# Masked queries as weights for the decode states, and page queues written out with another order of requests

## The chip, the cores and the metric

One Trainium2 chip, one of its cores. TensorE does matmuls into PSUM, DVE (VectorE) and ACT (ScalarE) do elementwise work, POOL (GpSimd) and SP (SyncE) mostly issue DMAs here. The metric is the device time of one launch in microseconds.

## The reference

One step of a small decoder trunk with two layers, for a prompt of 512 tokens and, with the same weights, for 8 decode sequences of 4 new tokens each. Every layer is a half-weighted SwiGLU, a mixer and a second half-weighted SwiGLU, each behind an RMS norm. Two parts of the mixers matter here.

The even mixer holds an mLSTM with 4 heads of width 192. For a decode sequence it has a state matrix per head. With a the decay of a token, s the weights of the sequence's own new tokens, and den the normaliser:

```
num = einsum('bhts,bhse->bhte', s, vc) + a[..., None] * einsum('bhed,bhtd->bhte', c, qc)
h   = num / maximum(abs(den), exp(-mt))[..., None]
c_new = decay[..., None, None] * c + einsum('bhs,bhse,bhsd->bhed', wk, vc, kc)
```

The odd mixer is a sparse attention over 2048 past tokens, kept in pages of 128 rows that a page table points to; a row holds `[cmp_k, cmp_v, sel_k, sel_v]`. The compressed branch averages overlapping blocks of the cmp rows, scores them, and its probabilities choose the 16 blocks that the selected branch may see; a third branch sees a window of the last 512 rows.

## The kernel before, in words

All five engines run programs written out by hand, with semaphores between them; nothing plans the order but the order of the code.

**Decode states.** `pe_even_decode`, `act_even` and `dve_even` go over 32 states (n = 8 x head + sequence). A state is 192 x 192, held as 96 rows of 2 x 192. For each state TensorE transposes it with four 96 x 96 transposes into PSUM bank n % 2 (`flip_state`, L1155), two states ahead; ACT copies the result to `cT` (L1323, three buffers); TensorE then multiplies it with the four scaled queries of that sequence (L1200): the transposed state is the weights, the queries are four moving columns, and the product lands in PSUM bank 7, channels in partitions, beside the terms of the new tokens (L1171) that were put there first over zeros (L1164). L1173 and L1176 make the denominators in bank 2. Every four states, eight matmuls on four row tiles (L1193) form the update of four states, and DVE adds each to its decayed state (L1456), which GpSimd stores (L905). Behind the loop L1206 does the normaliser state n, DVE multiplies the numerators with `rdn` (L1459), and the output projection starts (L939).

The fp32 matmuls of this kernel appear as two instructions each in the profile, the transposes as one.

**Pairs of sequences.** `pe_odd` takes the 8 decode sequences in four pairs (`pe_pair`, i = 0 to 3). Of the pages of a pair, SP loads those of the first sequence and GpSimd those of the second, 16 pages each, and of each page three parts apart: cmp rows (128 KB), selected keys (64 KB) and selected values (64 KB); GpSimd also loads the windows. One buffer holds one pair, so a part is asked for again when it has been read: the cmp rows after `pe_compress_pair` (L1921, counted by `sums_done`), the keys after the flips of the selected keys (L1949, `tk_done`), windows and values after the last product (L2011, `pvs_done`). TensorE's order within pair i is: scores of compressed rows, five flips of keys with their scores (L1949, L1972; the fifth reads the windows), then the compression of pair i+1 (L1921) with its transposes (L1928), then the transposes of the probabilities (L1989) and the products with the values (L2006, L2011). DVE picks the blocks and masks (L2269 to L2286); ACT takes the exponential (L2117), and does the copies for the compression of pair i+1 (L2098, L2100) ahead of the exponential of the selected scores.

The two queues before run this loop (GpSimd's, in `pool_odd`; SP's in `load_keys` is the same without the windows):

```python
            with po.Fori(0, NB // 2 - 1) as i:
                page = page_numbers(po, i + 1, 1)
                po.wait_ge(sums_done, i + 1)
                # cmp rows of pair i + 1
                po.wait_ge(tk_done, i * 5 + 4)
                # selected keys of pair i + 1
                po.wait_ge(pvs_done, i + 1)
                # windows, then selected values, of pair i + 1
```

`page_numbers` reads 16 entries of the page table into registers (L1686); its address is computed from the loop register. The first pair's numbers are read by SP one at a time at fixed addresses (L1707). `load_page` is L1691, `load_windows` L1697.

Of the kernel before, what the change touches and what calls it, by code (L numbers as in the profile page):

```python
# [22 lines left out]
SEQ = 512  # L23
# [47 lines left out]
def make_consts():  # L71
# [21 lines left out]
    put("onehot4", np.eye(4))  # L93
    put("round_mask", ((p[:, None] % 32) // NT == 4 * np.arange(2)[None, :] + p[:, None] // 32))
# [82 lines left out]
def trunk(nc, x_prompt, x_sample, state_pool, state_mlstm_c, state_mlstm_n, state_mlstm_m,  # L177
# [6 lines left out]
    with ctx:  # L184
# [530 lines left out]
        cT = [hf[:, 384 * i:384 * i + 384].rearrange("p (d e) -> p d e", d=2) for i in range(3)]  # L715
# [3 lines left out]
        aq, qna, rdn, qd = N.take(6, TS), N.take(6, TS), N.take(6, TS), N.take(2 * H4, TS)  # L719
# [30 lines left out]
        EMS, QD, WS_EXP = 1, 2, 3  # L750
# [74 lines left out]
        def pool_even(po, C):  # L825
# [57 lines left out]
            for hd in range(H4):  # L883
                po.wait_ge(cp_ready, hd + 1)
                if hd > 0:
                    po.wait_ge(cp_stored, 32 * hd)
                c = c_new_p[hd % 2]
                po.dma_start(c_p[0, 0, hd].rearrange("(e p) d -> p e d", p=EC),
                             c[0:EC].rearrange("p (e d) -> p e d", e=2)).then_inc(cp_stored, 16)
                po.dma_start(n_p[0, 0, hd].rearrange("(o d) -> o d", o=1), c[EC:EC + 1, DH:2 * DH]).then_inc(cp_stored, 16)  # L890

# [226 lines left out]
        def pe_even_decode(pe):  # L1118
# [25 lines left out]
            def flip_state(n):  # L1144
# [7 lines left out]
                for e in range(2):  # L1152
                    for d in range(2):
# [9 lines left out]
            pe.wait_ge(cp_ready, H4)  # L1163
            pe.matmul(ps[:, 7, 0:192], ident, const("zeros")[:, 0:1].broadcast_to([128, 192]), start=True, stop=False,  # L1164
                      skip_group_check=True)
            for hd in (0, 2, 1, 3):
# [3 lines left out]
                for c, a, b, e in pieces(hd):  # L1170
                    pe.matmul(ps[a:b, 7, 32 * c:32 * c + 32], vtok[0:TS, 4, DH * hd + e:DH * hd + e + b - a], wts[0:TS, hd],  # L1171
                              start=False, stop=False, skip_group_check=True)
# [5 lines left out]
            mm.then_inc(dd_done, 1)  # L1178
            pe.wait_ge(ktok_ready, 8)
            pe.wait_ge(yp_ready, 2 * H4)  # L1180
            pe.wait_ge(dact_ready, QD)
            for n in range(NB * H4):
# [3 lines left out]
                if b % 4 == 0:  # L1186
# [10 lines left out]
                pe.wait_ge(cT_ready, n + 1)  # L1197
                for c, a, bb, e in pieces(hd):
                    for d in range(2):
                        mm = pe.matmul(ps[a:bb, 7, 32 * c + NT * b:32 * c + NT * b + NT], cT[n % 3][0:EC, d, e:e + bb - a],  # L1200
                                       qd[0:EC, 2 * hd + d, NT * b:NT * b + NT], start=False, stop=(d == 1),
                                       skip_group_check=True)
                mm.then_inc(cq_done, 1)
            pe.wait_ge(cT_ready, NB * H4)
            for hd in range(H4):
                mm = pe.matmul(ps[0:NB, hd // 2, DH * (hd % 2):DH * (hd % 2) + DH], wkb[0:TS, hd], ktokd[0:TS, DH * hd:DH * hd + DH],  # L1206
                               start=True, stop=True)
# [3 lines left out]
        def act_even(act):  # L1211
# [82 lines left out]
            for hd in range(H4):  # L1294
# [4 lines left out]
                if hd >= 2:  # L1299
# [10 lines left out]
                           scale=-1.0).then_inc(dact_ready, 1)  # L1310
            pair = lambda v, i, n: v.rearrange("p (b i) t -> p b i t", i=n)[:, :, i, :]
            for dst, to, src, at, n in ((0, 0, 0, 0, 96), (1, 0, 0, 96, 32), (1, 32, 1, 0, 32), (1, 64, 1, 32, 32),
                                        (2, 0, 1, 64, 64), (2, 64, 2, 0, 32), (3, 0, 2, 32, 32), (3, 32, 2, 64, 32),
                                        (3, 64, 2, 96, 32)):
                q = act.copy(pair(qd, dst, 4)[to:to + n], pair(aq, src, 3)[at:at + n])
# [3 lines left out]
            for n in range(NB * H4):  # L1319
                act.wait_ge(ct_done, n + 1)  # L1320
                if n >= 3:
                    act.wait_ge(cq_done, n - 2)
                act.copy(cT[n % 3][0:EC], ps[0:EC, n % 2, 0:2 * DH].rearrange("p (d e) -> p d e", d=2)).then_inc(cT_ready, 1)  # L1323


        def dve_even(dve, C):
# [124 lines left out]
            for n in range(NB * H4):  # L1451
# [6 lines left out]
            dve.wait_ge(cq_done, NB * H4)  # L1458
            dve.tensor_tensor(ogT[:, :, SEQ:T], rdn, ps[:, 7, 0:192].rearrange("p (c t) -> p c t", c=6), ALU.mult  # L1459
                              ).then_inc(ddve_ready, 1)  # L1460
            dve.wait_ge(dd_done, 3)
            for hd in range(H4):
                dve.scalar_tensor_tensor(out=nS[0:NB, hd], in0=nS[0:NB, hd], scalar=dec_b[0:NB, hd:hd + 1],
                                         in1=ps[0:NB, hd // 2, DH * (hd % 2):DH * (hd % 2) + DH],
                                         op0=ALU.mult, op1=ALU.add).then_inc(ddve_ready, 1)
            dve.wait_ge(ddve_ready, Y_DEC + H4)
# [116 lines left out]
        def pool_odd(po, C):  # L1583
# [4 lines left out]
            po.wait_ge(zeroed, 7)  # L1588
# [49 lines left out]
            with po.Fori(0, NB // 2 - 1) as i:  # L1638
                page = page_numbers(po, i + 1, 1)
                po.wait_ge(sums_done, i + 1)  # L1640
                po.sem_inc(waited, 1)
                for g in range(NPG):
                    load_page(po, page[g], 1, g, 0, 256, cmp_in_b)
                po.wait_ge(tk_done, i * 5 + 4)
                po.sem_inc(waited, 1)
                for g in range(NPG):
                    load_page(po, page[g], 1, g, 256, 384, selk_in_b)
                po.wait_ge(pvs_done, i + 1)
                po.sem_inc(waited, 1)
                load_windows(po, i + 1)  # L1650
                for g in range(NPG):
                    load_page(po, page[g], 1, g, 384, 512, selv_in_b)

# [46 lines left out]
        def load_keys(sp):  # L1700
# [10 lines left out]
            with sp.Fori(0, NB // 2 - 1) as i:  # L1711
                page = page_numbers(sp, i + 1, 0)
                sp.wait_ge(sums_done, i + 1)
                sp.sem_inc(waited, 1)
                for g in range(NPG):
                    load_page(sp, page[g], 0, g, 0, 256, cmp_in)
                sp.wait_ge(tk_done, i * 5 + 4)
                sp.sem_inc(waited, 1)
# [700 lines left out]
```

## Time and profile before

| | us |
|---|---|
| median of 3 runs | 2811.13 (2810.02 to 2821.05) |
| profiled execution | 2811.16 |
| its span, first to last instruction | 2809.5 |
| TensorE busy in the span | 2591.4 (92%) |
| POOL, DVE, ACT busy | 308.5, 916.6, 611.8 |
| decode states, L1164 to the output projection | 717 to 815 |
| four pairs of sequences | 2076 to 2299 |

The rest of the span is feed-forward parts and projections, which the diff does not touch. Line numbers are those of the kernel before; x4 behind an operation is a number of instructions; `<-` names what an engine waited for. PEclk is the granted clock of TensorE, 1.00 being 2.4 GHz and 0.50 being 1.2 GHz. A busy TensorE counts pipelined matmuls, so its share says little of how full it is.

### The profile page before, as it was taken

Reading aid. Unit: us, or ns where it says so; the run is one execution under the profiler, and the core shown is the slowest. Engines: PE = TensorE matmul, PEld = TensorE weight load, DVE = VectorE, ACT = ScalarE, POOL = GpSimd, SP = SyncE. Lnnn points to the kernel's source line nnn. Section 1 sums busy time; section 2 is a strip of 40 time slices with the busy share of each in tenths; the row PEclk is TensorE's granted clock in tenths of the full one; section 3 lists DMA queues with packets and bytes.
Section 4 is the critical chain, followed back from the end, with each engine's and each line's share of the span. In section 5 each row is a group of like instructions: output and inputs, shape, how many; then the busy total and the mean of one; then the engine's idle time right before and its main releaser. Section 6 shows DMA issues by size and latency. Waiting matters only on the chain.

```text
span 2809.5 us, 45113 instructions
## 1 busy us (share of the span) xinstructions
PE 2591.4 (92%) x19104; PEld 2363.5 (84%) x19104; DVE 916.6 (33%) x1356; ACT 611.8 (22%) x883; POOL 308.5 (11%) x432
## 2 busy tenths in 40 slices
PE   7999998999998999998999998996975578999997
PEld 7999997996887999998999996764643357999997
DVE  4332326124213332334332332005652233332332
ACT  3211113222102211212211120013532112211122
POOL 0000002200210000000000002007664310000000
PEclk9999999999569999999999999997897789999998
DMA  5222222203113223222223212302134433223221
GB/s 166 78 80 90 79 72 94 90 16 91 37 50 105 90 67 112 68 68 90 90 68 112 79 57 77 123 23 82 41 102 139 135 76 89 90 75 105 90 63 44
DMA packets 220754, 232.07 MB, mean 83 GB/s; under 512 B 14650, under 2 KB 207467, under 8 KB 220425
## 3 DMA queue, kind: packets, MB, share of 16 engines
q1 hardware_dynamic: 209088, 199.51, 22.8%
q0 software_dynamic: 10912, 28.48, 3.2%
q8 instruction: 96, 1.57, 0.2%
q10 hardware_dynamic: 624, 2.23, 0.2%
q14 instruction: 34, 0.27, 0.0%
HBM read 220.87 MB, written 13.55 MB: 83 GB/s over the span
## 4 chain that ended last, share of the span: by engine, by line
PE 88%; DVE 4%; issue 2%; POOL 2%; ACT 2%; POOLq 1%; DMA 1%; DVEq 0%; SPq 0%; ACTq 0%
PE ps L351 57%; PE ps L953 6%; PE ps L939 4%; PE ps L926 2%; PE ps L919 2%; PE ps L1787 2%; PE ps L1200 2%; POOL ring L1661 1%; PE ps L1055 1%; PE ps L1861 1%; DVE ns L572 1%; POOLq L1686 1%; PE ps L1155 1%; PE ps L1890 1%; PE ps L1872 1%
## 5 line engine op out<-in xcount | busy, mean ns | idle before, releaser
L351 PE MATMUL ps<-h_hi,w_split 128*128 128x272 f32 x5632 | 941.5, 289 | 35.2 <-DVE h_lo L589 30.9
L351 PEld LDWEIGHTS ps<-h_hi,w_split 128*128 128x128 f32 x5632 | 800.3, 189 | 37.7 <-issue 37.7
L351 PE MATMUL ps<-h_lo,w_split 128*128 128x272 f32 x2816 | 586.1, 289 | 0.0
L351 PE MATMUL ps<-g_hi,w_split 128*128 128x272 f32 x2816 | 475.9, 289 | 0.0
L351 PEld LDWEIGHTS ps<-h_lo,w_split 128*128 128x128 f32 x2816 | 445.2, 190 | 0.0
L351 PEld LDWEIGHTS ps<-g_hi,w_split 128*128 128x128 f32 x2816 | 399.7, 188 | 1.9
L422 ACT CAST w_split<-ring 128x2048 fp32r<-128x2048 f32 (+2 forms) x148 | 247.5, 1672 | 388.7 <-PE ps L351 388.7
L429 DVE TENSOR_TENSOR w_split<-ring,w_split 128x2048 fp32r<-128x2048 f32 (+2 forms) x152 | 305.1, 2007 | 48.0 <-ACT w_split L422 47.9
L351 PE MATMUL ps<-g_lo,w_split 128*128 128x272 f32 x1408 | 291.1, 288 | 0.0
L465 DVE TENSOR_TENSOR ns<-ns,ps 128x544 f32<-128x544 f32 x88 | 63.5, 721 | 677.9 <-ACT ns L443 677.9
L443 ACT ACTIVATE ns<-ps 128x544 f32<-128x544 f32 x88 | 55.0, 625 | 786.9 <-PE ps L351 786.9
L351 PEld LDWEIGHTS ps<-g_lo,w_split 128*128 128x128 f32 x1408 | 221.4, 189 | 0.0
L487 DVE SCALAR_TENSOR_TENSOR x<-ps,x 128x544 f32<-128x544 f32 x64 | 46.4, 725 | 349.0 <-PE ps L351 349.0
L953 PE MATMUL ps<-h_hi,w_split 128*128 128x272 f32 (+1 forms) x864 | 148.1, 292 | 9.7 <-DVE h_lo L589 8.0
L953 PEld LDWEIGHTS ps<-h_hi,w_split 128*128 128x128 f32 (+1 forms) x864 | 122.4, 188 | 12.8 <-issue 8.6
L1661 POOL TENSOR_SCALAR ring<-ring,arena_t 128x128 f32<-128x128 f32 (+3 forms) x96 | 102.9, 1089 | 43.1 <-DVE arena_t L2178 42.9
L939 PE MATMUL ps<-arena_t,ring 128*128 128x272 f32 x448 | 105.9, 397 | 1.4 <-DVEq L2148 1.4
L939 PEld LDWEIGHTS ps<-arena_t,ring 128*128 128x128 f32 x448 | 86.2, 193 | 19.8 <-DVEq L2148 1.6
L1586 POOL MEMSET arena_t<- 128x18 f32 (+3 forms) x4 | 1.0, 290 | 913.2 <-DVE h L576 913.2
L953 PE MATMUL ps<-h_lo,w_split 128*128 128x272 f32 (+1 forms) x432 | 90.5, 291 | 0.0
L513 ACT ACTIVATE ns<-x 128x544 f32<-128x544 f32 x56 | 36.3, 654 | 210.6 <-DVE x L500 143.3
L1691 POOL DMA_DIRECT2D pages_t<-in_cache_nsa_kv_dram x144 | 77.2, 537 | 43.6 <-issue 37.8
(386 smaller groups left out, 2347.3 us busy)
## 6 DMA issues: line engine op xcount, KB each, us to landing
ring<-in_w_ffn_in_dram SPq DMA_DIRECT2D x88, 1024.0 KB, 7.6
ring<-in_w_ffn_out_dram SPq DMA_DIRECT2D x48, 768.0 KB, 5.0
ring<-in_w_in_even_dram SPq DMA_DIRECT2D x13, 1024.0 KB, 5.4
pages_t<-in_cache_nsa_kv_dram SPq DMA_DIRECT2D x80, 128.0 KB, 2.3
pages_t<-in_cache_nsa_kv_dram SPq DMA_DIRECT2D x160, 64.0 KB, 4.2
ring<-in_w_ffn_out_dram SPq DMA_DIRECT2D x16, 512.0 KB, 5.8
ring<-in_w_in_odd_dram SPq DMA_DIRECT2D x8, 768.0 KB, 5.7
pages_t<-in_cache_nsa_kv_dram POOLq DMA_DIRECT2D x48, 128.0 KB, 4.9
```

Source lines behind the costliest of these rows:

```text
L351: mm = pe.matmul(ps[:, b + s, 0:HALF], w, v[:, HALF * s:HALF * s + HALF], start=first and q == 0, stop=last and q == 2)
L422: act.copy(hi, raw).then_inc(split_hi, 1)
L429: dve.tensor_tensor(lo, raw, hi.bitcast(F32), ALU.subtract).then_inc(split_lo, 1)
L465: dve.tensor_tensor(halves(sil[u]), halves(sil[u]), banks(4 * u + 2), ALU.mult).then_inc(up_free, 1)
L919: mm = pe.matmul(ps[0:m, b + s, 0:HALF], w[:, k, cols:cols + m], h[:, k, HALF * s:HALF * s + HALF], start=(k == 0), stop=(k == NK - 1))
L926: mm = pe.matmul(out, h[:, k, 128 * t:128 * t + tok_tile(t)], w[:, k, lo:hi], start=(k == 0), stop=(k == NK - 1))
L939: mm = pe.matmul(ps[:, 4 * u + 2 * c + s, 0:HALF], w[0:rows_k, k, 128 * c:128 * c + 128], r[:, HALF * s:HALF * s + HALF], start=(k == 0), ...
L953: mm = pe.matmul(ps[0:rows_m, 4 * u + 2 * c + s, 0:HALF], w[:, k, 128 * c:128 * c + rows_m], v[:, k, HALF * s:HALF * s + HALF], start=(k = ...
L1200: mm = pe.matmul(ps[a:bb, 7, 32 * c + NT * b:32 * c + NT * b + NT], cT[n % 3][0:EC, d, e:e + bb - a], qd[0:EC, 2 * hd + d, NT * b:NT * b + ...
L1661: po.tensor_scalar(e, e, coef[:, s // 2 % 4, 2 * br + g:2 * br + g + 1], None, ALU.mult).then_inc(scaled, 1)
L1691: eng.dma_start(pages[:, b, g, lo:hi], cache_nsa_kv[0, ds(page, 1)].rearrange("a k r g d -> (a k) (r g d)")[:, lo:hi]).then_inc(landed, 16)
L1787: mm = pe.matmul(ps[64 * g:64 * g + 64, 4 + 2 * (p % 2) + s, 0:HALF], v[:, g, k, at:at + 64], h[:, k, HALF * s:HALF * s + HALF], start=(k ...
```

## The change

**Decode states.** The scaled queries are written into `q_all`, a zeroed part of `qT`, so that each sequence has a block of 32 columns in which only its own four are filled. These blocks become the weights: for four states at a time, `query(g)` runs eight matmuls, each 192 columns of a transposed state, on four column tiles, one per state. A row of the result belongs to a token, and PSUM bank 7 (heads 0 and 1) and bank 2 (heads 2 and 3) hold four partial results of 32 tokens each. `own_tokens` puts zeros and the terms of the new tokens there, once before the loop and once before the fifth group. `cT` gets eight buffers. A group's query runs behind the outer products of the next four states. At the end ACT copies the two banks to `y_tok`, and six matmuls with the constant `fold` add the four parts and put channels back into partitions; the n states are done before that. GpSimd zeroes `q_all` after the scores of the last head are done.

**Page queues.** Both loops are written out, so page table addresses are constants, and the order of the requests changes as the diff shows. SP's queue (not shown) changes in the same way, with `sp` for `po`, its own semaphores and no windows. The counts of `zeroed` rise from 7 to 8.

```diff
+    put("fold", (p[:, None] % 32) == np.arange(32)[None, :])
...
-        cT = [hf[:, 384 * i:384 * i + 384].rearrange("p (d e) -> p d e", d=2) for i in range(3)]
+        cT = [hf[:, 384 * i:384 * i + 384].rearrange("p (d e) -> p d e", d=2) for i in range(8)]
+        q_all = qT[:, 0:4, 0:2 * NB * 32]
+        q_of = q_all.rearrange("p h (d b t) -> p h d b t", d=2, b=NB)
+        y_tok = [kT[:, i, 0:2 * DH] for i in range(2)]
...
-        aq, qna, rdn, qd = N.take(6, TS), N.take(6, TS), N.take(6, TS), N.take(2 * H4, TS)
+        aq, qna, rdn = N.take(6, TS), N.take(6, TS), N.take(6, TS)
...
+                if hd == 2:
+                    po.wait_ge(s_done, 3 * H4)
+                    po.memset(q_all, 0.0).then_inc(zeroed, 1)
...
-            pe.wait_ge(cp_ready, H4)
-            pe.matmul(ps[:, 7, 0:192], ident, const("zeros")[:, 0:1].broadcast_to([128, 192]), start=True, stop=False,
-                      skip_group_check=True)
...
                 for c, a, b, e in pieces(hd):
-                    pe.matmul(ps[a:b, 7, 32 * c:32 * c + 32], vtok[0:TS, 4, DH * hd + e:DH * hd + e + b - a], wts[0:TS, hd],
-                              start=False, stop=False, skip_group_check=True)
                     pe.matmul(ps[a:b, 2, 32 * c:32 * c + 32], ones[0:TS, 0:b - a], wts[0:TS, hd],
                               start=True, stop=False, skip_group_check=True)
...
+
+            def own_tokens(i):
+                pe.matmul(ps[:, (7, 2)[i], 0:2 * DH], ident, const("zeros")[:, 0:1].broadcast_to([128, 2 * DH]),
+                          start=True, stop=False, skip_group_check=True)
+                for u in range(2):
+                    hd = 2 * i + u
+                    pe.matmul(ps[0:TS, (7, 2)[i], DH * u:DH * u + DH], wts[0:TS, hd],
+                              vtok[0:TS, 4, DH * hd:DH * hd + DH], start=False, stop=False, skip_group_check=True)
+
+            def query(g):
+                hd, q = g // 2, g % 2
+                if g == 4:
+                    pe.wait_ge(ddve_ready, RDN)
+                    own_tokens(1)
+                pe.wait_ge(cT_ready, 4 * g + 4)
+                for d in range(2):
+                    for r in range(4):
+                        mm = pe.matmul(ps[32 * r:32 * r + 32, (7, 2)[hd // 2], DH * (hd % 2):DH * (hd % 2) + DH],
+                                       q_of[0:EC, hd, d, 4 * q + r], cT[(4 * g + r) % 8][0:EC, d, :],
+                                       start=False, stop=(d == 1), tile_position=(0, 32 * r), skip_group_check=True)
+                mm.then_inc(cq_done, 1)
+
             pe.wait_ge(ktok_ready, 8)
+            pe.wait_ge(cp_ready, H4)
+            own_tokens(0)
...
             pe.wait_ge(dact_ready, QD)
-            for n in range(NB * H4):
+            for n in range(NB * H4 + 1):
...
-                if b % 4 == 0:
+                if b % 4 == 0 and n < NB * H4:
...
-                pe.wait_ge(cT_ready, n + 1)
-                for c, a, bb, e in pieces(hd):
-                    for d in range(2):
-                        mm = pe.matmul(ps[a:bb, 7, 32 * c + NT * b:32 * c + NT * b + NT], cT[n % 3][0:EC, d, e:e + bb - a],
-                                       qd[0:EC, 2 * hd + d, NT * b:NT * b + NT], start=False, stop=(d == 1),
-                                       skip_group_check=True)
-                mm.then_inc(cq_done, 1)
+                if n % 4 == 0 and n > 0:
+                    query(n // 4 - 1)
             pe.wait_ge(cT_ready, NB * H4)
             for hd in range(H4):
                 mm = pe.matmul(ps[0:NB, hd // 2, DH * (hd % 2):DH * (hd % 2) + DH], wkb[0:TS, hd], ktokd[0:TS, DH * hd:DH * hd + DH],
+                               start=True, stop=True)
+            mm.then_inc(dd_done, 1)
+            pe.wait_ge(dact_ready, Y_TOK + 1)
+            for c in range(6):
+                mm = pe.matmul(ps[:, 7, 32 * c:32 * c + 32], y_tok[c // 3][:, 128 * (c % 3):128 * (c % 3) + 128], const("fold"),
                                start=True, stop=True)
             mm.then_inc(dd_done, 1)
 
...
+            act.wait_ge(zeroed, 3)
...
+            def q_to(i, to, n):
+                v = qT[to:to + n, 0:4, 256 * (i % 2):256 * (i % 2) + NB * 36].rearrange("p (h u) s -> p h u s", u=2)[:, :, i // 2]
+                return v.rearrange("p h (b s) -> p h b s", s=36)[:, :, :, 0:NT]
...
-                q = act.copy(pair(qd, dst, 4)[to:to + n], pair(aq, src, 3)[at:at + n])
+                q = act.copy(q_to(dst, to, n), pair(aq, src, 3)[at:at + n].rearrange("p h (b t) -> p h b t", b=NB))
...
             for n in range(NB * H4):
                 act.wait_ge(ct_done, n + 1)
-                if n >= 3:
-                    act.wait_ge(cq_done, n - 2)
-                act.copy(cT[n % 3][0:EC], ps[0:EC, n % 2, 0:2 * DH].rearrange("p (d e) -> p d e", d=2)).then_inc(cT_ready, 1)
+                if n >= 8 and n % 4 == 0:
+                    act.wait_ge(cq_done, n // 4 - 1)
+                act.copy(cT[n % 8][0:EC], ps[0:EC, n % 2, 0:2 * DH].rearrange("p (d e) -> p d e", d=2)).then_inc(cT_ready, 1)
+                if n == 23:
+                    act.wait_ge(cq_done, 4)
+                    act.copy(y_tok[0], ps[:, 7, 0:2 * DH]).then_inc(dact_ready, 1)
+            act.wait_ge(cq_done, 8)
+            act.copy(y_tok[1], ps[:, 2, 0:2 * DH]).then_inc(dact_ready, 1)
...
-            dve.wait_ge(cq_done, NB * H4)
-            dve.tensor_tensor(ogT[:, :, SEQ:T], rdn, ps[:, 7, 0:192].rearrange("p (c t) -> p c t", c=6), ALU.mult
-                              ).then_inc(ddve_ready, 1)
...
+            dve.wait_ge(dd_done, 4)
+            dve.tensor_tensor(ogT[:, :, SEQ:T], rdn, ps[:, 7, 0:192].rearrange("p (c t) -> p c t", c=6), ALU.mult
+                              ).then_inc(ddve_ready, 1)
...
             po.wait_ge(pair_free, 1)
             load_windows(po, 0)
-            with po.Fori(0, NB // 2 - 1) as i:
-                page = page_numbers(po, i + 1, 1)
-                po.wait_ge(sums_done, i + 1)
-                po.sem_inc(waited, 1)
-                for g in range(NPG):
-                    load_page(po, page[g], 1, g, 0, 256, cmp_in_b)
-                po.wait_ge(tk_done, i * 5 + 4)
-                po.sem_inc(waited, 1)
+            LAST = NB // 2 - 1
+            page = page_numbers(po, 1, 1)
+            po.wait_ge(sums_done, 1)
+            for g in range(NPG):
+                load_page(po, page[g], 1, g, 0, 256, cmp_in_b)
+            for i in range(1, LAST + 1):
+                po.wait_ge(tk_done, 5 * i - 1)
                 for g in range(NPG):
                     load_page(po, page[g], 1, g, 256, 384, selk_in_b)
-                po.wait_ge(pvs_done, i + 1)
-                po.sem_inc(waited, 1)
-                load_windows(po, i + 1)
+                if i < LAST:
+                    page_next = page_numbers(po, i + 1, 1)
+                    po.wait_ge(sums_done, i + 1)
+                    for g in range(NPG):
+                        load_page(po, page_next[g], 1, g, 0, 256, cmp_in_b)
+                po.wait_ge(pvs_done, i)
+                load_windows(po, i)
                 for g in range(NPG):
                     load_page(po, page[g], 1, g, 384, 512, selv_in_b)
+                page = page_next
```

## Rows read from the trace of the kernel before

**Rows 1.** Chain of waits, 708 to 818 us: start, us, engine, line

```profile
715.74 1.45 PE ps L1155 x8
717.19 0.90 PE ps L1164 x2
718.09 0.56 PE ps L1171 x2
...
719.08 1.13 PE ps L1176 x4
720.20 0.34 PE ps L1171 x2
...
732.38 1.54 PE ps L1193 x16
...
735.39 0.81 PE ps L1155 x4
736.19 1.22 PE ps L1200 x8
...
810.85 2.67 PE ps L1206 x8
...
813.55 1.39 DVE pages_t L1463 x4
```

**Rows 2.** Groups by line, 708 to 818 us: busy us, mean ns, idle before

```profile
L1200 PE MATMUL ps<-ns,h 96*64 96x4 f32 (+1 forms) x256 | 47.7, 301 | 0.0
...
L1456 DVE SCALAR_TENSOR_TENSOR pages_t<-pages_t,ns,ps 96x384 f32<-96x384 f32 x32 | 18.2, 607 | 54.7 <-PE ps L1193 50.2 <-PE ps L1155 4.4
L1323 ACT COPY h<-ps 96x384 f32<-96x384 f32 x32 | 15.2, 475 | 75.2 <-PE ps L1155 75.2
L1193 PE MATMUL ps<-h,ns 32*96 32x192 f32 x128 | 12.9, 549 | 0.0
...
L888 POOL DMA_DIRECT2D out_dram<-ring x1 | 0.7, 655 | 8.3 <-ACT ring L1301 8.3
```

**Rows 3.** Busy time by stretch, decode states: span, engines, clock, DMA share, GB/s

```profile
713.00:732.30 19.30, 19.18 (x98) 16.17 (x96) 1.45 (x6) 3.07 (x11) 0.00 (x0) 0.50 0.00 1
732.30:810.90 78.60, 78.60 (x502) 69.14 (x502) 20.09 (x36) 14.26 (x30) 23.43 (x36) 0.50 0.21 61
```

**Rows 4.** TensorE's waits, 2070 to 2300 us: total us, times, longest

```profile
PE ps L1921 <- DMA pages_t<-in_cache_nsa_kv_dram: 50.8, 3, 22.4
```

**Rows 5.** Timeline of TensorE, pair 1: start, us, work, idle before

```profile
2161.90 6.96 PE L1921 MATMUL ps<-pages_t,arena_t 128*32 128x256 f32 x76 [21.44 <-DMA pages_t<-in_cache_nsa_kv_dram]
```

**Rows 6.** Timeline of GpSimd, pairs 1 and 2

```profile
2125.95 1.50 POOL L1697 DMA_DIRECT2D ring<-in_state_win_kv_dram  x2 [16.20 <-PE ps L2011]
...
2147.28 9.30 POOL L1691 DMA_DIRECT2D pages_t<-in_cache_nsa_kv_dram  x16 [10.82 <-issue]
...
2188.10 1.50 POOL L1697 DMA_DIRECT2D ring<-in_state_win_kv_dram  x2 [21.16 <-PE ps L2011]
```

**Rows 7.** Busy time by stretch around L1921 of pair 1, columns as rows 3

```profile
2162.00:2166.50 4.50, 4.50 (x44) 2.34 (x47) 0.00 (x0) 0.00 (x0) 3.31 (x7) 0.50 1.11 282
2166.50:2173.00 6.50, 3.02 (x41) 1.67 (x33) 0.12 (x1) 3.19 (x4) 0.43 (x1) 0.97 0.12 33
```

**Rows 8.** Timeline of DVE, end of the block choice of pair 1

```profile
2149.93 0.15 DVE L2286 TENSOR_SCALAR arena_t<-arena_t 128x1 f32<-128x1 f32 x1
```

**Rows 9.** Chain of waits, pair 1

```profile
2170.72 2.13 ACT ns L2117 x2
2172.99 2.98 PE ps L1989 x16
```

**Rows 10.** Instructions of lines L1686 and L1707: ns min/median/max

```profile
L1686 POOLq FUSED_REGOPS  x93: 46/152/187, 2077.8 to 2210.6; - x93
...
L1707 SPq FUSED_REGOPS  x32: 152/152/178, 1917.6 to 1987.5; - x32
```

More of the change, by code:

```diff
@@ L749, in trunk @@
         dact_ready, ddve_ready = sem("dact_ready"), sem("ddve_ready")
-        EMS, QD, WS_EXP = 1, 2, 3
+        EMS, QD, WS_EXP, Y_TOK = 1, 2, 3, 4
         AQ, QNA, WS_ARG, DEC, WS, RDN, Y_DEC = 1, 2, 3, 4, 5, 6, 7
@@ L1587, in pool_odd @@
                 mz.then_inc(zeroed, 1)
-            po.wait_ge(zeroed, 7)
+            po.wait_ge(zeroed, 8)
             n = 0
@@ L1710, in load_keys @@
                     load_page(sp, page, b, g, 384, 512, selv_in)
[L1711 to L1718, printed above, removed]
+            LAST = NB // 2 - 1
+            page = page_numbers(sp, 1, 0)
+            sp.wait_ge(sums_done, 1)
+            for g in range(NPG):
+                load_page(sp, page[g], 0, g, 0, 256, cmp_in)
+            for i in range(1, LAST + 1):
+                sp.wait_ge(tk_done, 5 * i - 1)
                 for g in range(NPG):
                     load_page(sp, page[g], 0, g, 256, 384, selk_in)
-                sp.wait_ge(pvs_done, i + 1)
-                sp.sem_inc(waited, 1)
+                if i < LAST:
+                    page_next = page_numbers(sp, i + 1, 0)
+                    sp.wait_ge(sums_done, i + 1)
+                    for g in range(NPG):
+                        load_page(sp, page_next[g], 0, g, 0, 256, cmp_in)
+                sp.wait_ge(pvs_done, i)
                 for g in range(NPG):
                     load_page(sp, page[g], 0, g, 384, 512, selv_in)
+                page = page_next
         crow_stored = sem("crow_stored")
@@ L2037, in act_odd @@
                 if p == 0:
-                    act.wait_ge(zeroed, 7)
+                    act.wait_ge(zeroed, 8)
                 for g in range(2):
```

## The prediction

> **What bounds the kernel now.** I read the chain of waits first, in two places that the diff touches. Around the decode states of the even layer (708 to 815 us) every step of the chain belongs to TensorE: the first state transposes, a zeroing matmul, the token terms, then per four states one group of outer products, and per state one group of transposes (L1155) and eight instructions of query product (L1200) [rows 1]. No other engine sets the pace: a DVE state update takes 607 ns and an ACT copy 475 ns [rows 2], where one state costs TensorE about 2.0 us (0.81 + 1.22). The table by stretch adds that the granted clock is 0.50, the 1.2 GHz level, from 713 us to the end of the loop, although TensorE counts as busy all the time [rows 3].
>
> The second place is the loop over four pairs of sequences in the odd layer (2076 to 2299 us). There TensorE waits 50.8 us in three waits before L1921, the compression of the next pair's rows, each for a page transfer [rows 4]; the wait inside pair 1 is 21.4 us [rows 5], the one inside pair 2 is 22.4, so that inside pair 0 is 7.0. GpSimd's queue shows why: after the last product of a pair (L2011) it issues two window loads in 1.5 us, then the values of sixteen pages, then reads sixteen page numbers, which leaves it 10.8 us without an issue, and only then asks for the compressed rows, sixteen issues in 9.3 us [rows 6]. SP runs the same order for the other sequence with cheaper issues; the chain runs through GpSimd.
>
> **Part 1: decode states.** Removed: the 256 instructions of L1200, 47.7 us of busy time [rows 2]; the zeroing of 192 columns (0.90 us); and eight pairs of L1171, 0.56 us for the four wide ones and about 0.34 for the others, together 3.6 [rows 1]. Four-column products cannot use the array; the new form makes the masked query the weights and streams 192 state columns, four states at a time in four column tiles.
>
> I rebuild TensorE's path from 717.19 (start of the zeroing) to 814.94 (end of the DVE step after L1206, where the output projection starts), 97.8 us now.
>
> 1. The denominator terms that stay (L1173, L1176): from 717.19 to the first outer products at 732.38 it is 15.2 us; less 0.90, less 3.6 and less one state's transposes (0.7, item 3) leaves 10.0.
> 2. `own_tokens` twice. Zeroing 384 columns is priced at twice the 0.90 us row; two heads of two instructions with 192 columns at L1206's price, 2.67/8 = 0.33 us each, 1.3. That is 3.1 each, 6.2 for both. While the first runs, DVE computes the reciprocal that its updates need.
> 3. Transposes of 30 states. Standing alone, eight took 1.45 us, so 0.73 us a state: 21.9. They alternate two banks and wait for ACT's copy, 0.475 us, which is shorter, so they do not stall.
> 4. Eight groups of outer products, unchanged: 1.54 each, 12.3.
> 5. Eight groups of query products. No row shows this form at this clock. Each is sixteen instructions of 192 columns on four tiles, as an outer-product group is, only with column tiles in place of row tiles. Below it is bounded by the compression L1921, the same four column tiles with 256 columns: 44 instructions in 4.50 us at a clock of 0.50 [rows 7], 0.102 us each, so 0.077 for 192 columns, 1.2 a group. Above it is bounded by no overlap at all, sixteen times L1193's mean of 549 ns [rows 2], 8.8. The nearest row is the outer product's 1.54, which has the same shape: 12.3.
> 6. Change of tile form, sixteen times. In the loop the outer products follow the transposes without a gap in the chain [rows 1]; I still allow 0.25 us each, 4.0, and keep 0 as the other end.
> 7. Behind the loop: the last copy and its hand-over 0.6, L1206 2.7, the twelve fold instructions at L1176's 1.13/4 = 0.28, 3.4, and one DVE product of about 0.4: 7.1 against 4.1 now. The two copies to `y_tok` run on ACT, the first in mid-loop, the second under L1206.
>
> Sum 10.0 + 6.2 + 21.9 + 12.3 + 12.3 + 4.0 + 7.1 = 73.8, a gain of 24.0 us (28 with free changes of form). DVE's four updates (4 x 0.61) plus the outer products stay under the 6.2 us that four states now cost TensorE. The memset on GpSimd stands ahead of head 3's store; GpSimd sits idle for 8.3 us there [rows 2]. No row shows a memset of 2048 elements, and only above 8.3 us would it delay that store, which nothing on the path awaits. The nine masked ACT copies are as many and as large as the old ones and end before the loop: 0. If they were late, TensorE would stand at the wait for them before the loop.
>
> The chain of the old loop shows outer products and query products directly behind transposes, four row tiles and the whole array in turn, with no gap between them [rows 1]. The Trainium skill ("TensorEngine Tiling (Array Packing)", Key Properties) says that changing the tiling mode drains the engine, which speaks against a loop that now has three forms in it; it gives no figure. With a price for it (item 6) the sum is 73.8, without one 69.8.
>
> **Part 2: page queues.** Written out, each queue asks for the compressed rows of pair i+1 as soon as pair i's are summed, ahead of pair i's windows and values. Both queues wait on `tk_done`, the new order then puts page reads and sixteen issues behind it, and behind those the windows and values wait.
>
> Inside pair 1's stretch GpSimd waits 16.2 us for L2011 before the windows at 2125.95 [rows 6], so it is free at 2109.75. Sixteen reads (8.4 us, below) and sixteen issues (9.3) then end at 2127.5 instead of 2156.6. The last one needs some 5.3 us to land (2156.6 to the start of L1921 at 2161.90, [rows 5, 6]), so the rows are there before TensorE stops at 2140.5. What is late next is DVE's selection chain. It ends (L2286) at 2150.08 [rows 8]; the exponential behind it takes 2.13 us [rows 9], so the transposes L1989 can start at about 2152.3 instead of 2172.99: 20.7 us. The compression (7.0 us) and the steps from its end to the exponential (1.9 us, 2168.86 to 2170.72 [rows 5, 9]) fit between 2140.5 and 2150, under that chain. Pair 2 waits 1.0 us more now, so 21.7. Pair 0 asks no earlier, but its page addresses become constants: reading a number costs one register instruction of 152 ns (32 for 32 reads of L1707) instead of two (93 for 48 of L1686) [rows 10], so sixteen reads take 10.8 - 2.4 = 8.4 us. It gains between 0 and 2.4, since the transfers themselves are late there; I take 1.5. Pair 3 has no next pair. Sum 43.9.
>
> The windows are where it could be given back. GpSimd needs, for a pair, 1.5 + 3 x 9.3 + 8.4 = 38 us, against a pair of about 41.5 us (2125.95 to 2188.10, one pair's windows to the next one's [rows 6], less 20.7), so windows go out within 1.5 us of L2011, about as now. With reads at today's 10.8 us and issues stretched by full queues to 11 us each, it is 45: 3 us late per pair, about 10 in all. I take 0.
>
> **Sum.** 24.0 + 43.9 = 67.9 us. The profiled execution took 2811.2 us (span 2809.5), equal to the median 2811.1 of the runs. 2811.2 - 67.9 = 2743.3, so 2743.
>
> **Rivals.**
> The clock comes back in the state loop. For it: the column-tiled L1921 ran 4.5 us at 0.50, and the stretch behind shows 0.97 [rows 7]; the new query products have that tile form. Against: the transposes of 96 columns and the outer products ran at 0.50 all through the old loop [rows 3], and they are still two thirds of the new one (34 of 54 us). At 1.00 TensorE's part halves, and DVE's four updates of 0.61 with outer products of 0.77 set 3.5 to 4 us per four states in place of 6.2: some 20 us less, 2723.
>
> The page queue becomes the bound: windows and values late behind the compressed rows, priced above at 10 to 15 us: 2756.
>
> Slower than before: the column tiles do not overlap and every query instruction pays its own latency. At 549 ns each the 128 instructions cost 70 us instead of 12.3, 2801, and it is a tie; from 0.63 us each the kernel is slower, from 0.74 by 0.5%. Against it stands L1921, where column tiles do overlap (0.102 us each).
>
> The change does nothing for pages: if the queue reached the compressed rows no earlier, because the waits in front of them end late, only part 1 is left, 2787. The order of the waits in the code speaks against it: `sums_done` of the pair is met inside the pair before.
>
> **How the numbers follow.** Forecast 0.55; clock 0.24; page queue 0.11; no overlap 0.06; nothing from pages 0.04. About 0.5%, 14 us, is what can be told from no change, so faster means under 2797: all cases but the no-overlap one, which splits, 0.04 same, 0.02 slower. The range reaches down to the clock rival with free changes of form, query groups at 1.2 and all of pair 0's 2.4 us: 2743 - 20 - 4 - 3 - 1 = 2715. Upwards it takes the queue rival's 10, no gain in pair 0 and query groups of twice the price taken, two tiles at a time: 2743 + 10 + 1.5 + 12 = 2767. Left out are the last two cases, 0.10, and some of the tails.
>
> **What would show it.** Decode stretch from 717 to the output projection about 74 us; query groups near 1.5 us; clock 0.50. In the pairs no wait of L1921 in pairs 1 and 2, ACT's exponential released by L2286, L1989 about 2.2 us behind it, a pair about 42 us; windows issued within 2 us of L2011. Wrong if the clock row reads 1.00 there, if L1193's successor waits, or if TensorE waits for windows or values.

## The result, and the profile after

The changed kernel takes 2736.5 us, median of four runs (2724.9 to 2737.4), against 2816.1 for four of the kernel before: ratio 0.9707, 95% interval 0.9669 to 0.9745. The forecast was 2743, the range 2715 to 2767. Time and range were met; the path to them was not the forecast one. The profiled execution took 2724.9 us (span 2723.2), 86.2 less than that of before, where 67.9 were forecast.

The two traces part at the same places of the code. The kernel before, timeline of TensorE, the pairs' marks that did not stand above:

```profile
2112.64 3.42 PE L1989 MATMUL ps<-cst,ns 128*128 128x128 f32 x16 [2.78 <-ACT ns L2117]
...
2237.77 2.90 PE L1989 MATMUL ps<-cst,ns 128*128 128x128 f32 x16 [2.79 <-ACT ns L2117]
...
2299.12 11.12 PE L939 MATMUL ps<-arena_t,ring 128*128 128x272 f32 x40 [1.42 <-DVEq L2148]
```

The changed kernel, the same view (L1966 is the old L1921, L2034 the old L1989, L946 the output projection):

```profile
2057.72 5.80 PE L1966 MATMUL ps<-pages_t,arena_t 128*32 128x256 f32 x76 [5.24 <-DMA pages_t<-in_cache_nsa_kv_dram]
2067.65 3.37 PE L2034 MATMUL ps<-cst,ns 128*128 128x128 f32 x16 [2.79 <-ACT ns L2162]
...
2095.36 4.52 PE L1966 MATMUL ps<-pages_t,arena_t 128*32 128x256 f32 x76
2107.36 3.65 PE L2034 MATMUL ps<-cst,ns 128*128 128x128 f32 x16 [6.13 <-ACT ns L2162]
...
2150.93 3.65 PE L2034 MATMUL ps<-cst,ns 128*128 128x128 f32 x16 [6.14 <-ACT ns L2162]
...
2213.05 2.22 PE L946 MATMUL ps<-arena_t,ring 128*128 128x272 f32 x6 [1.41 <-DVEq L2193]
```

The waits before the compression are gone in pairs 1 and 2, and 5.24 us are left in pair 0. The chain of waits shows what is late instead, DVE's selection and then ACT's exponential, as forecast:

```profile
2146.12 2.33 DVE arena_t L2330
...
2148.47 0.17 DVE arena_t L2331
...
2148.66 2.13 ACT ns L2162 x2
...
2150.93 3.65 PE ps L2034 x16
```

Decode states, the changed kernel, chain of waits: the first denominator product, the own tokens, two outer-product groups (L1219), query products (L1198), transposes (L1162), the tail:

```profile
721.85 0.56 PE ps L1175 x2
...
732.91 1.44 PE ps L1183 x2
734.35 1.41 PE ps L1187 x4
735.76 0.81 PE ps L1162 x4
736.57 1.54 PE ps L1219 x16
...
742.62 0.48 PE ps L1162 x4
...
743.13 0.48 ACT h L1355
...
743.65 0.91 PE ps L1162 x8
744.57 0.83 PE ps L1219 x16
745.40 0.79 PE ps L1198 x16
746.19 0.48 PE ps L1162 x4
...
767.90 1.39 PE ps L1227 x8
769.29 1.92 PE ps L1232 x12
...
771.70 28.30 PE ps L946 x111
```

Busy time by stretch, columns as in [rows 3]:

```profile
717.00:738.90 21.90, 21.78 (x112) 16.56 (x111) 3.66 (x9) 3.62 (x13) 0.00 (x0) 0.50 0.00 1
738.90:767.90 29.00, 26.43 (x360) 17.55 (x359) 17.26 (x32) 12.98 (x30) 22.45 (x35) 0.99 0.50 149
```

The granted clock, 0.50 all through the old loop [rows 3], is back to 1.00 from the second group on; in the two further traces of this kernel (below) the second group still runs at 0.50 and the third at 1.00. The difference of the profiled executions, stretch by stretch, from these marks and [rows 1, 9]:

| stretch | before | after | forecast | measured |
|---|---|---|---|---|
| start of L1164, now of L1175 | at 717.2 | at 721.9 | 0 | +4.7 |
| decode path, to the output projection | 97.8 | 49.9 | -24.0 | -47.9 |
| from there to the transposes of pair 0 | 1297.7 | 1296.0 | -1.5 | -1.7 |
| pair 0 to pair 1 | 60.4 | 39.7 | -20.7 | -20.6 |
| pair 1 to pair 2 | 64.8 | 43.6 | -21.7 | -21.2 |
| pair 2 to the output projection | 61.4 | 62.1 | 0 | +0.8 |

The first row belongs to this execution: around 630 us, in code that did not change, the clock fell to 0.73.

```profile
625.00:650.00 25.00, 25.00 (x92) 16.21 (x91) 5.43 (x13) 11.36 (x26) 5.99 (x5) 0.73 0.94 262
```

The two further traces of the same kernel read 1.00 there, but four traces of other kernels below read 0.67 to 0.73 (`states_only`, `no_query`, `query_later`, `den_spread_2`): this fall comes and goes, and why is not known.

### The profile page after: what moved, and what is told of

The parts are those of the page before. It is cut to its first block, busy times and chain, and to the rows that moved or that the text cites. A ratio compares the mean times of both kernels' runs of the same rounds, so it can differ in the third digit from the quotient of the medians.

```text
span 2723.2 us, 44701 instructions
## 1 busy us (share of the span) xinstructions
PE 2541.9 (93%) x18982; PEld 2314.0 (85%) x18982; DVE 915.1 (34%) x1356; ACT 612.1 (22%) x885; POOL 310.1 (11%) x432
## 4 chain that ended last, share of the span: by engine, by line
PE 89%; DVE 5%; POOL 2%; ACT 2%; issue 1%; DMA 0%; POOLq 0%; DVEq 0%; SPq 0%; ACTq 0%
PE ps L352 59%; PE ps L960 6%; PE ps L946 4%; PE ps L933 2%; PE ps L926 2%; PE ps L1832 2%; PE ps L1062 1%; POOL ring L1702 1%; PE ps L1906 1%; DVE ns L573 1%; PE ps L1917 1%; PE ps L1935 1%; PE ps L385 1%; PE ps L2051 1%; PE ps L551 1%
## 5 line engine op out<-in xcount | busy, mean ns | idle before, releaser
L946 PE MATMUL ps<-arena_t,ring 128*128 128x272 f32 x448 | 106.6, 399 | 1.4 <-DVEq L2193 1.4
L1702 POOL TENSOR_SCALAR ring<-ring,arena_t 128x128 f32<-128x128 f32 (+3 forms) x96 | 103.0, 1089 | 41.6 <-DVE arena_t L2223 41.3
L946 PEld LDWEIGHTS ps<-arena_t,ring 128*128 128x128 f32 x448 | 86.9, 194 | 19.9 <-DVEq L2193 1.6
```

The costliest lines, as they stand in the source:

```text
L946: mm = pe.matmul(ps[:, 4 * u + 2 * c + s, 0:HALF], w[0:rows_k, k, 128 * c:128 * c + 128], r[:, HALF * s:HALF * s + HALF], start=(k == 0), ...
L1702: po.tensor_scalar(e, e, coef[:, s // 2 % 4, 2 * br + g:2 * br + g + 1], None, ALU.mult).then_inc(scaled, 1)
```

## The experiments

"Path" is the stretch from the first denominator product (or the zeroing, where that comes first) to the output projection; "pairs" is from the transposes of pair 0 to the output projection behind pair 3, 186.5 us before and 145.4 after.

**Each part alone, the old order, and the changed kernel again.** `pages_only` and `states_only` each take one part of the diff.

> The kernel before with the page queues alone written out. Theory (the two parts add, and the page order is worth what the pairs lost in the changed kernel): the starts of L1989 stand 39.7, 43.6 and 43.8 us apart instead of 60.4, 64.8 and 43.0, and pair 0 wins 1 to 2 us, so 42 to 43 us under the kernel before, ratio about 0.985; the decode states as before, 97.8 us at a clock of 0.50. Rival (the page gain hangs on the earlier arrival from the shorter state loop): the pairs keep waits of 10 us or more before L1921 and the ratio is above 0.99.

> The kernel before with the decode states alone changed, the pairs as before. Theory (the new loop itself brings TensorE's clock back): the clock reads 0.50 up to the loop and 1.00 behind its first groups, the path from the denominator terms to the output projection is about 50 us instead of 97.8, ratio 0.982 to 0.985. Rival (the return of the clock in the one trace was a state of that execution, as the fall at 630 us was): the loop stays at 0.50, the path is about 74 us and the ratio 0.991.

`old_order`, GpSimd's queue (SP's changes in the same way):

```diff
             for i in range(1, LAST + 1):
+                page = page_numbers(po, i, 1)
+                po.wait_ge(sums_done, i)
+                for g in range(NPG):
+                    load_page(po, page[g], 1, g, 0, 256, cmp_in_b)
                 po.wait_ge(tk_done, 5 * i - 1)
...
-                if i < LAST:
-                    page_next = page_numbers(po, i + 1, 1)
-                    po.wait_ge(sums_done, i + 1)
-                    for g in range(NPG):
-                        load_page(po, page_next[g], 1, g, 0, 256, cmp_in_b)
                 po.wait_ge(pvs_done, i)
```

> The changed kernel with the page queues still written out, but in the old order: compressed rows of the next pair behind the windows and values of this one. Theory (the order makes the gain): three waits for compressed rows of together 45 to 51 us return, the time is 38 to 43 us above the changed kernel, ratio about 0.985 to the kernel before. Rival (the constants in place of a loop's register make it, by cheaper page reads and no loop turn): the waits stay under 10 us together and the ratio is about 0.971, as in the changed kernel.

> The changed kernel once more, unaltered, for a second trace. Theory: ratio 0.970 (0.967 to 0.974), the clock again 1.00 from the first groups of the state loop on; the 4.7 us that L1062 lost at a clock of 0.51 around 630 us belong to one execution and may be absent. Rival (the clock's return is a matter of the execution): the loop reads 0.50 and the profiled time is near 2749.

| kernel | ratio to before, 95% | path | pairs |
|---|---|---|---|
| `pages_only` | 0.987 (0.984 to 0.989) | 97.8 | 149.4 |
| `states_only` | 0.985 (0.982 to 0.988) | 51.4 | 186.7 |
| `old_order` | 0.984 (0.981 to 0.987) | 51.4 | 180.9 |
| `after_again` | 0.971 (0.968 to 0.974) | 51.4 | 149.6 |

The parts add: 0.987 x 0.985 = 0.972. The new loop shortens the path to 51.4 in every kernel that has it, so the clock's return is no accident of one trace. `old_order` has its three waits back, somewhat less than the 45 to 51 us expected, at the compression's line there:

```profile
PE ps L1954 <- DMA pages_t<-in_cache_nsa_kv_dram: 44.2, 3, 21.4
```

Its median is 32 to 36 us above those of the changed kernel, where 38 to 43 were expected. `states_only` differs from it only in the written-out loops: the pairs take 186.7 there and 180.9 here, so writing the loops out won about 6 us, and the order won the 31 to 36 us of the pairs that are left. The first trace's pairs were its best: 145.4, against 149.6 and, in `after_third`, 147.1. The difference lies between pairs 0 and 1 (39.7, 43.2, 41.6), where the clock over 2036 to 2096 us reads 0.94 in the first trace and 0.86 in the other two, which does not tell these two apart. The page part is thus worth 37 to 41 us between these marks; the profiled execution of `pages_only` is 38.0 us under that of the kernel before, where 42 to 43 were expected.

**What brings the clock back.** `no_query` leaves out the call of L1198, `old_no_query` the loop over L1200 in the kernel before, and `four_cols` adds this to the new loop (256 instructions, as in the old one):

```diff
+                if n < NB * H4:
+                    if n == NB * H4 // 2:
+                        pe.wait_ge(ddve_ready, RDN)
+                    pe.wait_ge(cT_ready, n + 1)
+                    for c, a, bb, e in pieces(hd):
+                        for d in range(2):
+                            pe.matmul(ps[a:bb, (7, 2)[hd // 2], 384 + NT * b:384 + NT * b + NT], cT[n % 8][0:EC, d, e:e + bb - a],
+                                      q_of[0:EC, hd, d, b, NT * b:NT * b + NT], start=(d == 0), stop=(d == 1),
+                                      skip_group_check=True)
                 if n % 4 == 0 and n > 0:
                     query(n // 4 - 1)
```

Its added products share the accumulators' banks, and the tokens' output of that layer changes with them.

> The changed kernel without the 128 query products of L1198 (the states' share of the tokens' output is left out; transposes, copies, outer products, updates and own tokens stay). Theory A (the four-column products of the old loop held TensorE at 0.50, and without them wide products bring it back): 1.00 within the first two groups of the loop, though no query product runs; a group of four states takes 2.6 to 2.9 us. Theory B (the query products with their four column tiles bring it back): the loop reads 0.50 throughout and a group takes 4.4 to 4.7 us.

> The kernel before without the 256 four-column products of L1200 (the states' share of the tokens' output is left out), all else as before: no own-token products of 192 columns ahead of the loop. Theory A (four-column products hold the clock down): 1.00 within the first groups, a group of four states under 3 us, the path from L1171 to the output projection 45 to 48 us. Theory C (the 384 and 192 columns wide products of own_tokens, directly ahead of the new loop, bring the clock back): 0.50 throughout, 4.5 us a group, the path 55 us or more.

> The changed kernel with the old loop's 256 four-column products added to the new loop, into columns of the accumulators that nobody reads, eight behind each state's transposes. Theory A (they hold the clock down): 0.50 through the loop, about 11 us per four states (4 x 0.81 + 4 x 1.22 + 1.54 + 1.44), path about 105 us. Theories B and C (wide products bring it back whatever else runs): 1.00 from the first groups on, 5.6 to 6 us per four states, path 65 to 70 us.

Busy time by stretch, `no_query`, whose clock rises at 749.6:

```profile
749.60:773.00 23.40, 19.54 (x209) 13.47 (x207) 14.89 (x28) 11.68 (x27) 19.80 (x31) 0.97 0.55 163
```

`old_no_query`, which has neither query nor own-token products, rises at 744:

```profile
713.00:744.00 31.00, 30.89 (x186) 25.05 (x187) 8.48 (x18) 7.75 (x22) 6.63 (x10) 0.50 0.14 39
744.00:762.30 18.30, 14.55 (x168) 10.21 (x166) 12.64 (x25) 9.00 (x21) 15.87 (x25) 1.00 0.58 171
```

`four_cols`, the whole loop, and one piece of its chain (L1229 is the added line):

```profile
731.30:828.10 96.80, 96.80 (x647) 76.60 (x647) 18.15 (x32) 15.14 (x32) 23.45 (x36) 0.50 0.17 50
```

```profile
741.99 1.54 PE ps L1219 x16
743.53 1.47 PE ps L1229 x8
745.00 1.44 PE ps L1198 x16
746.44 0.81 PE ps L1162 x4
747.24 1.22 PE ps L1229 x8
```

Theory A holds, B and C fall: transposes and outer products alone get the clock back, and the four-column products, put beside the same wide work, keep it at 0.50, though TensorE counts as busy for all 96.8 us. `four_cols` is one trace, but the loops of the kernel before and of `pages_only`, which have these products too, read 0.50 throughout as well. Paths: 46.6, 46.2 and 113.9 us; for the last about 105 was expected, because the four-column products were priced at 1.22 us a state, and many take 1.47. At full clock a group takes 3.3 us in both loops without query products, not under 3: the outer products wait for DVE's updates there. `no_query`, one group of the chain:

```profile
754.86 0.91 PE ps L1214 x16
...
756.88 1.14 DVE pages_t L1488 x2
...
758.15 0.91 PE ps L1214 x16
```

`four_cols` also prices the new forms at 1.2 GHz: a query group 1.44 us, directly behind outer products or four-column products, without a gap between forms.

**Can the loop be ordered better?** At full clock the chain has a new piece, 0.48 us of ACT's copy per group, and 11.1 us of narrow denominator products stand ahead of the loop at 0.50. `query_later` issues the query one state later; `den_spread` takes the denominators into the loop; `spread_later` does both.

```diff
-                if n % 4 == 0 and n > 0:
+                if n % 4 == 1 and n > 4:
                     query(n // 4 - 1)
...
+            DEN_AT = (5, 6, 7, 9, 10, 11, 13, 14)
...
+                if n in DEN_AT:
+                    denominator(DEN_AT.index(n))
```

> The changed kernel with the query products of each four states issued two transposes later (behind the second state's transposes instead of ahead of them), to fill the wait of 0.5 us for ACT's copy that each group shows since the clock is up. Theory: the wait goes, a group of four states takes 3.1 to 3.2 us instead of 3.57, the path from L1175 to the output projection 48 us instead of 51.4, the time 3 us less than the changed kernel's, which the runs alone can hardly tell. Rival (ACT's copies set the pace in any order): the wait turns up elsewhere in the group and the path stays at 51 us.

> The changed kernel with the denominator products L1175 and L1178 (48 instructions of 32 columns, 11.1 us at 0.50 ahead of the loop) spread over the states 5 to 14 of the loop, and DVE's reciprocal behind its update 15. Theory (in the loop's mixture 32 columns do not hold the clock as 4 columns did): the clock is up some 10 us after the first wide product, as before, so about 728 us; the products run at full clock and partly in the waits for ACT; path 43 to 46 us. Rival (narrow products hold the clock, of 32 columns too): 0.50 until state 15, path 54 to 58 us, slower than the changed kernel.

> Both edits of order together. Theory: path 41 to 45 us, the time 7 to 10 us under the changed kernel, ratio to the kernel before 0.967 to 0.968. Rival (narrow products hold the clock): path 52 us or more and ratio 0.971 or above.

`query_later`, chain of waits, one group at full clock:

```profile
756.80 0.48 PE ps L1162 x4
...
757.30 0.48 ACT h L1356
...
757.83 0.54 PE ps L1162 x4
758.36 0.84 PE ps L1219 x16
759.20 0.47 PE ps L1162 x4
759.67 0.79 PE ps L1198 x16
760.45 0.48 PE ps L1162 x4
```

The wait stays, between other transposes: a group takes 3.65 us (756.80 to 760.45) where the changed kernel takes 3.57 (742.62 to 746.19). The theory falls; the rival was right that the copy's wait only moves. The clock came back later, at 756 us, and the path is 55.0; ratio 0.971 (0.969 to 0.973).

`den_spread`, busy time by stretch; the last narrow product ends at 758.3:

```profile
719.20:758.30 39.10, 39.10 (x249) 27.16 (x249) 9.92 (x20) 9.32 (x23) 13.24 (x20) 0.50 0.21 61
758.30:792.00 33.70, 32.68 (x231) 20.03 (x229) 13.06 (x25) 7.89 (x17) 10.18 (x16) 0.50 0.25 71
```

The clock does not come back, path 69.7, ratio 0.9745 (0.971 to 0.978): the theory falls, and the rival's 54 to 58 was passed too, since the loop stayed at 0.50 beyond the narrow products. `spread_later`: 1.00 from about 763, path 59.7, ratio 0.971 (0.969 to 0.973), so its theory falls too. No order tried beats the changed kernel.

**The two again, for a second and a third trace.**

> The kernel with the denominator products spread over the loop, unaltered, for a second trace. In its first one the clock stayed at 0.50 to the end of the loop, 34 us beyond the last narrow product, with the same work behind it in which the changed kernel's clock came back. Theory (when the clock comes back differs between executions): this trace may show 1.00 in the second half of the loop, path 58 to 64 us instead of 69.7, and a time near 2735. Rival (narrow products in the loop's first half keep it down for good): 0.50 to the end again, path 69 to 70 us, time near 2750.

> The changed kernel, unaltered, for a third trace. Theory (the clock's return differs between executions and makes the spread of 2725 to 2739 us): a time near 2737 goes with a return later than 740 us or with a fall of the clock elsewhere, one near 2727 with a return at about 740. Rival (the spread comes from elsewhere, transfers for example): the state loop and the clock elsewhere are as in the first two traces though the time is near 2737.

`den_spread_2`, where the narrow products end at 764.2:

```profile
724.00:764.20 40.20, 40.14 (x255) 27.91 (x255) 9.93 (x20) 10.24 (x27) 13.25 (x20) 0.50 0.20 60
...
768.00:783.90 15.90, 13.57 (x179) 8.52 (x172) 9.66 (x17) 5.97 (x14) 9.33 (x15) 1.00 0.42 121
```

This time the clock came back, at 768, with the path at 60.2, as the theory had it. The time, 2746.4 us, did not follow to 2735: the loop begins 5.9 us later than in the first trace, behind the fall of the clock around 630 us, which this trace has and the first has not. So the same instructions regain the clock in one trace and not in another. The two traces come from two chips, so a difference between chips is not ruled out; but of the first chip's four executions one took 2735.4 us at a mean granted clock of 0.952, the other three 2748 to 2751 at 0.945 to 0.946, which speaks for a difference between executions.

That products of 32 columns hold the clock down fits `den_spread_2` and `spread_later`, where it comes back 4 and 10 us behind the last of them, but it is not shown: in `den_spread` it stays down for 34 us without them, and in `query_later`, with none in the loop, it came back only at 756.

`after_third` took 2728.2 with the path at 51.4 again. No trace fell on an execution near 2737, so where in the span its 12 us lie is open. They go with the clock: the executions of this kernel of 2725 to 2729 us have a mean granted clock of 0.954 to 0.957, those of 2736 to 2739 us 0.949 to 0.951. The kernel before has the same spread, 2809 to 2822 us at 0.939 to 0.933, so the new loop is not needed for it.

## Why the prediction was right or wrong

**Page queues: right.** 43.9 us forecast, 42.8 in the first trace, and with the pairs' 36.9 and 39.4 of the other two, and 1.3 to 1.6 less wait in pair 0, some 38 to 41. Place and order were as said: no wait of L1921's successor in pairs 1 and 2, the exponential released by DVE's selection, the transposes 2.3 us behind it (2148.6 to 2150.9). From pair 1 to pair 2 it is 43.6, where a pair of about 42 was said. The wait in pair 0 went from 6.9 to between 5.2 and 5.6, near the 1.5 taken. Off by a little: the stretch behind pair 2 takes 0.7 to 1.1 us more, sixteen page reads take GpSimd 8.8 to 9.1 us instead of 8.4, and the windows leave 2.7, 1.7 and 0.3 us behind L2056 (the old L2011), where 2 at most was said. The timeline of GpSimd after, the loop's first two requests for windows:

```profile
2073.55 9.30 POOL L1732 DMA_DIRECT2D pages_t<-in_cache_nsa_kv_dram  x16 [9.10 <-issue]
2082.84 1.50 POOL L1738 DMA_DIRECT2D ring<-in_state_win_kv_dram  x2
...
2123.83 1.50 POOL L1738 DMA_DIRECT2D ring<-in_state_win_kv_dram  x2 [1.48 <-issue]
```

The queue rival's mechanism is seen in the first of them, sixteen requests in front of the windows, but TensorE waited for no window and no value, so no cost of it shows.

**Decode states: the terms right, the clock wrong.** `den_spread` is nearly the forecast case, the same work at 0.50 to the end: 69.7 us where the sum said 73.8, and 69.8 with free changes of form; so close a match is partly luck, since single items are off by about 1 us either way. Item by item in the changed kernel, at 0.50: denominators 11.1 (10.0 forecast), own tokens 2.85 (3.1), four transposes 0.72 a state (0.73), outer products 1.54 (1.54), query products 1.44 (1.54), changes of form next to nothing (4.0). Of the tiling rule that was weighed: the Trainium skill ("TensorEngine Tiling (Array Packing)", Key Properties) has the engine drain at a change of tiling mode, and here outer products, query products and transposes follow one another in the chain with no gap. The chain's matmul ends are modelled, so a small price could sit inside the pieces: one state's transposes between other forms read 0.81 us, in a run of sixteen 0.72. That leaves about 0.1 us where 0.25 was allowed, and the item was too large. The memset on GpSimd took 1.82 us, under its bound of 8.3.

The step that failed is the one against the clock rival: "the transposes of 96 columns and the outer products ran at 0.50 all through the old loop", and so would hold it down in the new. They ran at 0.50 because of the four-column products beside them, as `old_no_query` and `four_cols` show: without these products the same transposes and outer products rise to 1.00, with them they stay at 0.50. The rival's own reason was wrong as well: it gave the query products' tile form the credit, and `no_query` rises without a query product, as `old_no_query` does. Its price was good, 53.8 for the path against 51.4, and 2723 for the kernel against 2725 in the profiled execution, though its pace has another source: ACT's copy between transposes ends the wait in each group, not DVE's updates; the chain runs through DVE in the loops without query products.

That the time came out so near the forecast is luck. Between the two profiled executions the gain was 86.2 us, where 67.9 were forecast: the states gave 46 to 48 us instead of 24, the pages about 1 less than said, and the fall of the clock at 630 us took back 4.7. The median of 2736.5 lies nearer to 2743 because three of its four executions are about 12 us longer than the traced one, while the forecast started from a short execution of the kernel before.

**The other rivals.** Column tiles overlap: sixteen query instructions in 1.44 us at 1.2 GHz and 0.79 at 2.4, 0.09 and 0.05 each, far below the 0.63 at which the kernel would have been slower. The pages did gain.

## What to carry to other kernels

Work that streams few columns can cost more than its own rows. The 256 four-column instructions held 44.0 us of the old chain, 1.22 us in 12 of the 32 states and 1.47 in 20, as in the second of these lines of the kernel before:

```profile
757.35 0.71 PE ps L1155 x4
758.07 1.47 PE ps L1200 x8
```

Taking them out shortened the path by 51.6 us, although a part of the new path is waits for DVE and ACT, because the work beside them had run at 1.2 GHz. So a granted clock read off a stretch belongs to the whole mixture, and it must not be carried over to a stretch from which one of the ingredients is taken. In a queue that serves several buffers, put first the request whose data is awaited first: here the order gave 31 to 36 us, and writing the loops out about 6.

## What was not expected of the hardware

TensorE at 100% busy can stay at 1.2 GHz for as long as the loop runs: 96.8 us with four-column products in it (busy all the time), and in `den_spread` the whole path of 70 us, though products of 32 columns run in only 24 of them (734.3 to 758.3). And whether the clock comes back is not settled by the instructions alone: with the same ones it read 0.50 to the end of the loop in one trace and 1.00 over the last 16 us of it in another. What decides between the two was not found.
